# One 32-token expert item moved from the second expert group into the first, two blocks behind its 96-token item

## The chip, the cores and the metric

The kernel runs on one core of a Trainium2 chip. The metric is the device time of one execution in microseconds (us), lower is better. Before the change it took 2199.92 us (median of 3 runs, 2199.86 to 2200.71).

## The reference

The program is a chain of two transformer blocks over 256 tokens of width 1024. The change touches one step of it, the mixture of experts at the end of the first block:

```
def _moe(h, router, w1, w3, w2):
    hf = h.reshape(b * t, d)
    logits = (hf @ router).astype(jnp.float32)
    top_v, top_i = lax.top_k(logits, TOP_K)            # TOP_K = 2
    top_w = jax.nn.softmax(top_v, axis=-1)
    gates = jnp.sum(jax.nn.one_hot(top_i, N_EXPERTS) * top_w[..., None], axis=-2)
    y = jnp.zeros_like(hf)
    for e in range(N_EXPERTS):                         # 8 experts, D_EXPERT = 3584
        y = y + gates[:, e:e + 1] * _swiglu(hf, w1[e], w3[e], w2[e])
    return y.reshape(b, t, d)
```

`_swiglu` is (silu(h w1) * (h w3)) w2. Everything is in f32. Each token goes to two of the eight experts, so the kernel gathers for each expert the tokens that chose it and computes those alone. Which expert has many tokens and which few is known only on the chip.

## The kernel before

**Items and halves.** An item is one expert with room for a number of tokens. The eight experts are ranked by load, and item number i takes the expert whose rank is `SLOT_PLACE[i]`, with room `PLACE_CAPS`. In the code a room of 96 is `MIDDLE`, 160 is `LARGE`, 64 is `LOW`, 32 is `SMALL`. An expert's weights are 42 MiB, and they are streamed from HBM in 42 pieces of 1 MiB that the code calls halves. Halves 0 to 23 of an item belong to blocks 0 to 2 of w1 and w3 (8 halves a block: 4 of w1, 4 of w3), halves 24 to 27 to the short block 3, and halves 28 to 41 to w2 (the downs). The tokens are the stationary operand, 32 columns at a time, and the weights are the moving one. So PE's time for a half grows with the room of the item, and the time of its transfer doesn't.

**Places.** SyncE (SP) issues the halves in the order in which they are used, into 14 places of 1 MiB (`half`, L898). The transfer of half n waits until half n-14 has been used (`s_half_used`). In this document the halves of the whole stage are numbered through from 0: 336 of them, 42 for each of eight items.

**Groups.** Four groups and a last item are worked off in turn:

| group | items before | halves |
|---|---|---|
| first | 96 | 0 to 41 |
| second | 96 and 32 | 42 to 125 |
| third | 160 and 32 | 126 to 209 |
| fourth | 96 and 64 | 210 to 293 |
| last | 96 (a loop, here one pass) | 294 to 335 |

A group of two items takes block 0 of its first item, block 0 of its second, block 1 of the first and so on, and the downs by fives in turn (`order`). Within it PE does other work at fixed halves: the turning of the `put` table (L1371, after half 4 of a group), the turning of the inner values of each block, needed for w2 (`turn`, L1386 to L1390, two or three halves after a block), the gather of the next group's tokens into PSUM (`gather`, L979, after the 6th down half) and the scatter of the previous group's output (`scatter`, L1362, after half 1 of a group). ACT copies gathered tokens to SBUF (`tokens`, L1998), DVE makes the tables for the next group (`select`), and both do silu and the products between up and down.

Up products are at L1435 (rooms or parts of 64) and L1439 (parts of 32), the down products at L1460 and L1464.

Of the kernel before, what the change touches and what calls it, by code (L numbers as in the profile page):

```python
# [11 lines left out]
ALU = mybir.AluOpType  # L12
# [27 lines left out]
SLOT_PLACE = (0, 2, 6, 1, 7, 3, 5, 4)  # L40
# [46 lines left out]
def block_halves(block):  # L87
    return 8 if block < UP_BLOCKS - 1 else 4
# [16 lines left out]
class Group:  # L105
# [10 lines left out]
    put_parts: int  # L116

# [19 lines left out]

    def order(self):

        out = []  # L140
        for block in range(UP_BLOCKS):
            for j in range(len(self.members)):
                out += [(j, 8 * block + m) for m in range(block_halves(block))]
# [12 lines left out]

    def event(self, block, p):

        return block * len(self.parts()) + p

    def cross(self, block, p):

        small = self.small_parts()
        return block * len(small) + small.index(p)
# [4 lines left out]
    def turn_before(self, block, p):  # L169

        own = self.event(block, p)
        users = [self.event(b, q) for b in range(block + 1) for q in range(len(self.parts())) if self.turn[q] == self.turn[p]]
        return max((u for u in users if u < own), default=None)
# [5 lines left out]
def one(first, widths, up1, up3, turn, down, gathered=(0, 1), put_parts=None):  # L179
# [4 lines left out]
GROUPS = (one(0, MIDDLE, (0, 1), (2, 3), (4, 5), (6, 7), (6, 7)),  # L184
          Group(1, (MIDDLE, SMALL), (0, 1, 1), (2, 3, 3), (4, 5, 4), (7, 2, 3), (2, 3, 4, 5), (0, 1), (2, 3, 2), 3),
# [4 lines left out]
FLUSH_AT, ADD_AT, PUT_AT, PUT_SB_AT, SELECT_AT, GATHER_AFTER = 1, 3, 4, 5, 12, 5  # L190

# [189 lines left out]
def build(nc, A, out):  # L381

    with ExitStack() as ctx:
# [17 lines left out]
        s_silu_zero = sem("silu_zero")  # L401
# [29 lines left out]
        s_pad_zero = sem("pad_zero")  # L431
# [67 lines left out]
        s_gather_ready = sem("gather_ready")  # L499
        s_xg_ready = sem("xg_ready")  # L500
# [9 lines left out]
        s_y_zero = sem("y_zero")  # L510
# [295 lines left out]
        def _(sp):  # L806
# [94 lines left out]
            for g, grp in enumerate(GROUPS):  # L901
                n0 = before(halves_of, g)
                if g == 1:
                    sp.wait_ge(s_items_ready, 2)
                ids = [0 if grp.first + j == 0 else
                       sp.value_load(item_list[0:1, grp.first + j:grp.first + j + 1], min_val=0, max_val=N_EXPERTS - 1)
                       for j in range(len(grp.members))]
# [64 lines left out]
        def _(pe):  # L972
# [42 lines left out]
            pe.wait_ge(s_ones_ready, 1)  # L1015
# [328 lines left out]
            def gather(g, grp):  # L1344

                pe.wait_ge(s_select_ready, g + 1)
                cap = grp.cap()
                per = grp.per_bank()
                for k in range(KT):
                    b, at = grp.gathered[k // per], cap * (k % per)  # L1350
                    mm = group(psum[:, b, at:at + cap], [(h_tok[:, t, k * P:(k + 1) * P], pick[:, t, 0:cap]) for t in range(2)])
                mm.then_inc(s_gather_ready, 1)

# [39 lines left out]
            def experts(g, grp, ev, cr, hv, arrived, previous, following):  # L1393
# [93 lines left out]
            gather(0, GROUPS[0])  # L1487
# [251 lines left out]
        def _(act):  # L1739
# [39 lines left out]
            act.wait_ge(s_silu_zero, 1)  # L1779
# [9 lines left out]
            act.wait_ge(s_ones_ready, 1)  # L1789
# [26 lines left out]
            act.wait_ge(s_pad_zero, 1)  # L1816
# [175 lines left out]
            def tokens(g, grp):  # L1992

                act.wait_ge(s_gather_ready, g + 1)
                cap, per = grp.cap(), grp.per_bank()
                for k in range(KT):
                    b, at = grp.gathered[k // per], cap * (k % per)
                    a = act.activation(x_full[:, k, 0:cap], psum[:, b, at:at + cap], ACT.Identity, bias=mod[:, 1, 24 + k, 0:1])  # L1998
                    if k % 2:
                        a.then_inc(s_xg_ready, 1)  # L2000

# [18 lines left out]
            def experts(g, grp, ev, cr, hv, previous, following):  # L2020

                parts = grp.parts()
                for at, (j, m) in enumerate(grp.order()):
# [24 lines left out]
                    for block in range(UP_BLOCKS):  # L2048
                        for q in range(len(parts)):
                            if at == grp.turn_at(block, q):  # L2050
                                inner_turned(grp, block, q, ev)
                    if at == grp.downs() + GATHER_AFTER and following:
                        tokens(g + 1, following)

            act.wait_ge(s_items_ready, 1)
            tokens(0, GROUPS[0])
# [169 lines left out]
        def _(dve):  # L2226
# [58 lines left out]
            dve.memset(silu_c[:, :, :], 0.0).then_inc(s_silu_zero, 1)  # L2285
# [89 lines left out]
            dve.wait_ge(s_pad_zero, 1)  # L2375
# [254 lines left out]
            for t in range(2):  # L2630
                for part, width in enumerate(MIDDLE):
                    x = select_put(t, part, width, 64 * part, rank8[:, t, 0:1], gate8[:, t, 0:1])
            x.then_inc(s_put_first, 1)
# [77 lines left out]
            dve.tensor_scalar(item_rank2, item_rank, float(P), None, ALU.subtract)  # L2711
            dve.tensor_scalar(sink8, pr("sinks"), 1.0 / SCALE2, None, ALU.mult)
# [26 lines left out]
            def experts(g, grp, ev, cr, hv, previous, following, following_first):  # L2739

                parts = grp.parts()
                for at, (j, m) in enumerate(grp.order()):
# [4 lines left out]
                    for block in range(UP_BLOCKS):  # L2747
                        width = sub_block(block)
                        for q in range(len(parts)):
                            done = grp.up_done(parts[q][0], block, 0)  # L2750
                            if at == done + 1 and parts[q][1] == 32:
                                dve.wait_ge(s_half_used, hv + done + 1)
                                s = grp.cross(block, q)
                                if s:
                                    last = (block, grp.small_parts()[-2]) if q == grp.small_parts()[-1] and len(grp.small_parts()) > 1 else (
                                        block - 1, grp.small_parts()[-1])
                                    dve.wait_ge(s_up_silu, ev + grp.event(*last) + 1)
# [19 lines left out]
            dve.wait_ge(s_y_zero, 1)  # L2777
# [255 lines left out]
        def _(pool):  # L3033
            pool.memset(apad, 0.0).then_inc(s_pad_zero, 1)
# [3 lines left out]
            pool.memset(y_T, 0.0).then_inc(s_y_zero, 1)  # L3038
# [148 lines left out]
```

## Time and profile before

| what | value |
|---|---|
| median of three runs | 2199.92 us |
| span of the profiled execution | 2198.8 us |
| PE busy over the span | 2113.4 us (96%) |
| the expert stage, first to last half on PE | 811.46 to 1688.60 us of the span |
| PE busy in the second group | 175.56 of 194.96 us |

Times in rows are microseconds from the span's start. Each matmul in f32 stands in the profile as two records, so a count of x16 in a profile row is eight matmuls of the program. Nearly 4 matmuls run beside each other, in different columns of the array, so the difference between the starts of two rows is the pace, and the busy time of a row is somewhat longer than that.

### The profile page before, as it was taken

How to read it: one execution, taken by the hardware profiler on the slowest of the kernel's cores; microseconds unless marked ns; L12 is line 12 of the kernel's file. 1: busy time of each engine (PE TensorE's matmuls, PEld its weight loads, DVE VectorE, ACT ScalarE, POOL GpSimd, SP SyncE). 2: the span in 40 equal slices, each digit the busy share in tenths (PEclk: the TensorE clock that was granted, in tenths of full speed). 3: DMA queues.
4: the chain of work that ended last, by engine and by line, in shares of the span. 5: the costliest groups of instructions: out<-in, count | busy, mean ns of one | idle time of the engine just before them, and what ended most of it. 6: DMA issues, size and time to landing. Idle time of an engine off the chain costs nothing.

```text
span 2198.8 us, 35772 instructions
## 1 busy us (share of the span) xinstructions
PE 2113.4 (96%) x15146; PEld 1315.2 (60%) x15146; DVE 859.6 (39%) x1582; ACT 548.2 (25%) x1019; POOL 89.9 (4%) x109
## 2 busy tenths in 40 slices
PE   5999999999999999999889999999999999999998
PEld 2655688888866673433333343333433877889998
DVE  4698632224543432032001210110022467666755
ACT  3214432224442420010000100000011134434443
POOL 0000000000000000000000000000501200001300
PEclk9999999999999999999999999999999999999999
DMA  9895232323111559999999999999995332344451
GB/s 370 324 360 214 77 99 93 106 85 105 57 63 51 203 195 373 358 383 402 418 413 409 385 401 382 404 402 418 412 407 210 128 116 77 115 154 174 174 188 58
DMA packets 160740, 536.71 MB, mean 244 GB/s; under 512 B 7120, under 2 KB 31824, under 8 KB 139728
## 3 DMA queue, kind: packets, MB, share of 16 engines
q1 hardware_dynamic: 160448, 534.08, 63.6%
q8 instruction: 109, 1.79, 0.3%
q0 software_dynamic: 144, 0.52, 0.1%
q14 instruction: 39, 0.32, 0.0%
HBM read 533.53 MB, written 1.05 MB: 243 GB/s over the span
## 4 chain that ended last, share of the span: by engine, by line
PE 84%; DVE 6%; DMA 5%; DVEq 3%; issue 1%; ACT 1%; SPq 0%; ACTq 0%
PE psum L1435 15%; PE psum L986 11%; PE psum L987 10%; PE psum L988 10%; PE psum L979 10%; PE psum L1439 7%; PE psum L1460 7%; PE psum L1464 3%; DMA X<-in_o_exp_w 2%; DVE region L2369 2%; DVEq L2372 1%; PE psum L1003 1%; DMA region<-in_o_exp_w 1%; PE psum L1362 1%; DMA ring<-in_o_exp_w 1%
## 5 line engine op out<-in xcount | busy, mean ns | idle before, releaser
L986 PE MATMUL psum<-region_r 128*128 128x512 f32 (+1 forms) x1392 | 480.5, 345 | 14.5 <-DVE H_lo L2356 3.5
L987 PE MATMUL psum<-region_r 128*128 128x512 f32 (+1 forms) x1280 | 431.2, 337 | 0.0
L988 PE MATMUL psum<-region_r 128*128 128x512 f32 (+1 forms) x1152 | 394.4, 342 | 0.0
L986 PEld LDWEIGHTS psum<-region_r 128*128 128x128 f32 x1392 | 264.1, 190 | 62.6 <-issue 22.1
L987 PEld LDWEIGHTS psum<-region_r 128*128 128x128 f32 x1280 | 243.0, 190 | 25.3
L988 PEld LDWEIGHTS psum<-region_r 128*128 128x128 f32 x1152 | 218.5, 190 | 25.5
L1435 PE MATMUL psum<-ring,region 128*32 128x512 f32 (+1 forms) x2064 | 203.5, 527 | 1.6 <-DMA ring<-in_o_exp_w 1.6
L1435 PEld LDWEIGHTS psum<-ring,region 128*32 128x32 f32 x2064 | 65.9, 111 | 118.5 <-issue 102.7
L979 PE MATMUL psum<-H,ring 128*128 128x256 f32 x576 | 128.7, 380 | 0.0
L2008 ACT ACTIVATE region<-psum 128x256 f32<-128x256 f32 (+2 forms) x56 | 24.8, 450 | 374.8 <-PE psum L1386 277.9
L979 PEld LDWEIGHTS psum<-H,ring 128*128 128x128 f32 x576 | 108.3, 190 | 16.5 <-ACT region L2084 1.3
L1435 PE MATMUL psum<-region 128*32 128x512 f32 (+1 forms) x1072 | 115.8, 562 | 0.0
L2722 DVE COPY rstd<-psum 128x512 f32<-128x512 f32 x5 | 3.5, 692 | 277.7 <-PE psum L1464 216.5
L2735 DVE COPY region<-psum 64x512 f32<-64x512 f32 (+1 forms) x56 | 35.1, 627 | 187.6 <-PE psum L1439 186.9
L2772 DVE TENSOR_TENSOR region<-region,psum 128x512 f32<-128x512 f32 (+1 forms) x28 | 17.0, 620 | 226.3 <-PE psum L1439 184.3
L1439 PE MATMUL psum<-ring,region 128*32 128x512 f32 (+1 forms) x912 | 98.4, 525 | 0.8 <-DMA ring<-in_o_exp_w 0.8
L2369 DVE SCALAR_TENSOR_TENSOR region<-region,param 128x512 f32<-128x512 f32 x120 | 84.8, 748 | 4.1 <-issue 0.4
L2453 DVE TENSOR_TENSOR region_r<-ring,region_r 128x512 fp32r<-128x512 f32 x88 | 58.7, 689 | 57.3 <-ACT region_r L1869 57.3
L1460 PE MATMUL psum<-ring,region 128*32 128x512 f32 x640 | 77.8, 618 | 2.8 <-DMA ring<-in_o_exp_w 2.8
L1439 PE MATMUL psum<-region 128*32 128x512 f32 (+1 forms) x584 | 70.0, 571 | 4.5 <-DMA region<-in_o_exp_w 3.9
L1435 PEld LDWEIGHTS psum<-region 128*32 128x32 f32 x1072 | 33.4, 110 | 66.3 <-issue 62.4
L1869 ACT ACTIVATE region_r<-ring 128x512 fp32r<-128x512 f32 x88 | 52.8, 627 | 63.6 <-PE psum L988 63.4
(403 smaller groups left out, 2719.0 us busy)
## 6 DMA issues: line engine op xcount, KB each, us to landing
ring<-in_o_exp_w SPq DMA_DIRECT2D x151, 1024.0 KB, 12.7
region<-in_o_exp_w SPq DMA_DIRECT2D x118, 1024.0 KB, 14.3
ring<-in_w_ada SPq DMA_DIRECT2D x24, 2048.0 KB, 10.6
H<-in_o_exp_w SPq DMA_DIRECT2D x46, 1024.0 KB, 14.9
ring<-in_w_ff SPq DMA_DIRECT2D x16, 2048.0 KB, 8.0
ring<-in_e_ffn_w SPq DMA_DIRECT2D x22, 1024.0 KB, 7.8
X<-in_o_exp_w SPq DMA_DIRECT2D x21, 1024.0 KB, 14.4
ring<-in_w_in SPq DMA_DIRECT2D x10, 2048.0 KB, 8.2
```

What stands on the lines that cost most here:

```text
L979: mm = pe.matmul(dst, lhsT, rhs, start=(i == 0), stop=(i == len(pairs) - 1))
L986: pe.matmul(out, a_hi, b_hi, start=first, stop=False)
L987: pe.matmul(out, a_hi, b_lo, start=False, stop=False)
L988: mm = pe.matmul(out, a_lo, b_hi, start=False, stop=last)
L1435: mm = pe.matmul(psum[r:r + 32, to, 0:width], x_full[:, k, slot0 + 32 * tg:slot0 + 32 * tg + 32], moving, start=(k == 0), stop=(k == KT - 1))
L1439: mm = pe.matmul(psum[r:r + 32, to, 0:width], x_full[:, k, slot0:slot0 + 32], moving, start=(k < 2), stop=(k >= KT - 2))
L1460: mm = pe.matmul(psum[r:r + 32, grp.down[q], :], he[:, i, slot0 + 32 * tg:slot0 + 32 * tg + 32], moving, start=(i == 0), stop=(i == ET - 1))
L1464: mm = pe.matmul(psum[r:r + 32, grp.down[q], :], he[:, i, slot0:slot0 + 32], moving, start=(i < 2), stop=(i >= ET - 2))
L1869: act.activation(fw_hi[:, u % SPLIT, :].rearrange("p (k w n) -> p k w n", k=2, w=2), up_unit(cs, u), ACT.Copy).then_inc(s_ffn_hi, 1)
L2369: x = dve.scalar_tensor_tensor(conv[i], apad[:, i, :, k:k + T], taps[:, i, k:k + 1], conv[i], ALU.mult, ALU.add)
L2453: dve.tensor_tensor(lo, up_unit(cs, u), hi.bitcast(F32), ALU.subtract).then_inc(s_ffn_lo, 1)
L2735: dve.tensor_copy(cross_sum[0:64, to, 0:width], psum[64:128, b, 0:width])
```

## The change

The second group's 32-token item goes into the first group, and the second group is left with its 96-token item alone. The ranks of items 1 and 2 are swapped in `SLOT_PLACE`, so that the same experts keep the same rooms. The first group is now 96 and 32, with halves 0 to 83, the second 96, with halves 84 to 125. From half 126 on nothing is moved.

In the first group the second item is two blocks behind (`lag` 2): blocks A0, A1, A2, then B0, A3, B1, B2, B3 (A the 96-token item, B the 32-token one), then the downs by fives as before. B's tokens get a gather of their own after half 12, into PSUM bank 6 (`gather_second`), with a copy by ACT (`tokens_second`) and tables made by DVE behind the planning of the items, after which DVE now reports `s_put_first`. DVE's `select` for the next group waits for that gather too. SP reads B's expert number when it comes to half 24. Some semaphores are merged to make room for two new ones.

```diff
-SLOT_PLACE = (0, 2, 6, 1, 7, 3, 5, 4)
+SLOT_PLACE = (0, 6, 2, 1, 7, 3, 5, 4)
+    def up_order(self):
+        steps = [(j, step - self.lag * j) for step in range(UP_BLOCKS + self.lag) for j in range(len(self.members))]
+        return [(j, block) for j, block in steps if 0 <= block < UP_BLOCKS]
-GROUPS = (one(0, MIDDLE, (0, 1), (2, 3), (4, 5), (6, 7), (6, 7)),
-          Group(1, (MIDDLE, SMALL), (0, 1, 1), (2, 3, 3), (4, 5, 4), (7, 2, 3), (2, 3, 4, 5), (0, 1), (2, 3, 2), 3),
+GROUPS = (Group(0, (MIDDLE, SMALL), (0, 1, 1), (2, 3, 3), (4, 5, 4), (7, 2, 3), (2, 3, 4, 5), (6, 7), (2, 3, 2), 3, 2),
+          one(2, MIDDLE, (0, 1), (2, 3), (4, 5), (7, 2)),
+SECOND_AT, SECOND_BANK = 12, 6
...
+                    if g == 0 and (j, m) == (1, 0):
+                        sp.wait_ge(s_items_ready, 2)
+                        ids[1] = sp.value_load(item_list[0:1, 1:2], min_val=0, max_val=N_EXPERTS - 1)
...
+            def gather_second(grp):
+                slot0, cap = sum(grp.members[0]), grp.cap()
+                width = cap - slot0
+                pe.wait_ge(s_put_first, 1)
+                for k in range(KT):
+                    mm = group(psum[:, SECOND_BANK, width * k:width * k + width],
+                               [(h_tok[:, t, k * P:(k + 1) * P], pick[:, t, slot0:cap]) for t in range(2)])
+                mm.then_inc(s_second_gather, 1)
...
+                    if grp.lag and (j, m) == (1, 0):
+                        pe.wait_ge(s_second_xg, 1)
...
+                    if at == SECOND_AT and grp.lag:
+                        gather_second(grp)
...
+            def tokens_second(grp):
+                act.wait_ge(s_second_gather, 1)
+                for k in range(KT):
+                    a = act.activation(x_full[:, k, slot0:cap], psum[:, SECOND_BANK, width * k:width * k + width], ACT.Identity,
+                                       bias=mod[:, 1, 24 + k, 0:1])
+                a.then_inc(s_second_xg, 1)
...
-            x.then_inc(s_put_first, 1)
...
+            for t in range(2):
+                x = dve.tensor_scalar(pick[:, t, slot0:cap], cn("iota")[:, 0:cap - slot0], item_rank[:, t, 1:2], item_mask[:, t, 1:2],
+                                      ALU.is_equal, ALU.mult)
+            for t in range(2):
+                x = select_put(t, len(MIDDLE), cap - slot0, 0, item_rank[:, t, 1:2], item_gate[:, t, 1:2])
+            x.then_inc(s_put_first, 1)
...
+                        if grp.lag:
+                            dve.wait_ge(s_second_gather, 1)
```

The first place is PE's stream around half 12 (`region`, `H` and `X` are places for weights; half 13 is in `H`). Before (L1435 and L1439 are the up products of one half):

```order
L1435 MATMUL psum<-region 32x512 x8
L1439 MATMUL psum<-region 32x512 x4
L1435 MATMUL psum<-region 32x512 x8
L1439 MATMUL psum<-region 32x512 x4
L1435 MATMUL psum<-H,region 32x512 x8
L1439 MATMUL psum<-H,region 32x512 x4
```

Now (the up products are L1462 and L1466, the gather's helper L993):

```order
L1462 MATMUL psum<-region 32x512 x8
L1466 MATMUL psum<-region 32x512 x4
L1462 MATMUL psum<-region 32x512 x8
L1466 MATMUL psum<-region 32x512 x4
L993 MATMUL psum<-region 128x32 x16
L1462 MATMUL psum<-H,region 32x512 x8
L1466 MATMUL psum<-H,region 32x512 x4
```

Sixteen matmuls with 32 moving columns have come in between halves 12 and 13 of the first group.

The second place is PE's stream from half 22 of the first group on, `ring` and `region` being places for the weights. Before, block 3 of the 96-token item (256 columns) follows its block 2:

```order
L1435 MATMUL psum<-ring,region 32x512 x8
L1439 MATMUL psum<-ring,region 32x512 x4
L1435 MATMUL psum<-ring,region 32x512 x8
L1439 MATMUL psum<-ring,region 32x512 x4
L1435 MATMUL psum<-ring,region 32x256 x16
L1439 MATMUL psum<-ring,region 32x256 x8
L1435 MATMUL psum<-region 32x256 x16
L1439 MATMUL psum<-region 32x256 x8
```

Now the eight halves of B0 stand between them, four matmuls each, with the turning of A2 (L1411 to L1415) after the second:

```order
L1462 MATMUL psum<-ring,region 32x512 x8
L1466 MATMUL psum<-ring,region 32x512 x8
L1466 MATMUL psum<-region 32x512 x4
L1411 MATMUL psum<-const,region 128x128 x4
L1466 MATMUL psum<-region 32x512 x4
L1413 MATMUL psum<-const,region 128x64
L1415 MATMUL psum<-const,region 128x64 x3
L1466 MATMUL psum<-H,region 32x512 x4
L1466 MATMUL psum<-X,region 32x512 x4
L1466 MATMUL psum<-H,region 32x512 x4
L1466 MATMUL psum<-region 32x512 x8
L1462 MATMUL psum<-region 32x256 x16
```

The first block of short halves, which followed half 49, now follows half 23.

## Rows read from the trace of the kernel before

**Rows 1.** Busy time by group (stretch, length, engines, granted clock, DMA share, GB/s).
```profile
811.46:929.96 118.50, 118.50 (x1172) 43.69 (x1176) 23.21 (x65) 13.23 (x32) 0.00 (x0) 1.00 0.95 353
929.96:1124.92 194.96, 175.56 (x1596) 61.59 (x1589) 34.65 (x64) 16.73 (x37) 0.00 (x0) 0.95 1.01 403
1124.92:1365.82 240.90, 240.22 (x2361) 88.84 (x2365) 34.47 (x62) 18.53 (x42) 0.00 (x0) 0.99 1.00 395
1365.82:1573.76 207.94, 207.19 (x2040) 79.72 (x2032) 24.87 (x45) 17.09 (x38) 25.62 (x42) 1.00 1.02 409
```
**Rows 2.** What PE waited for from 1126 to 1689 us (total, times, longest).
```profile
PE psum L1460 <- DVE region L2772: 0.7, 1, 0.7
```
**Rows 3.** PE timeline of the first group (start, length, line, shapes, count).
```profile
806.95 3.78 PE L979 MATMUL psum<-region 128*128 128x96 f32 x32
...
814.06 1.90 PE L1435 MATMUL psum<-H,region 128*32 128x512 f32 x16
...
816.63 1.90 PE L1435 MATMUL psum<-region 128*32 128x512 f32 x16
...
824.47 0.66 PE L1371 MATMUL psum<-const,region 128*128 128x128 f32 x4
...
877.06 1.91 PE L1435 MATMUL psum<-ring,region 128*32 128x256 f32 x32
...
905.57 3.84 PE L979 MATMUL psum<-region 128*128 128x128 f32 x32
```
**Rows 4.** SP timeline: issue of the transfer into the first freed place.
```profile
814.30 0.37 SPq L898 DMA_DIRECT2D X<-in_o_exp_w  x1
```
**Rows 5.** DMA issues from 857 to 877 us (KB, us from issue to landing).
```profile
ring<-in_o_exp_w SPq DMA_DIRECT2D x4, 1024.0 KB, 6.8
```
**Rows 6.** PE timeline of the second group, with idle time before a row and its releaser.
```profile
935.23 3.72 PE L1362 MATMUL psum<-region,rstd 64*128 64x256 f32 x32
...
946.74 0.87 PE L1371 MATMUL psum<-const,region 128*128 128x128 f32 x6
...
962.11 1.04 PE L1439 MATMUL psum<-X,region 128*32 128x512 f32 x8
962.97 1.04 PE L1439 MATMUL psum<-H,region 128*32 128x512 f32 x8
...
1022.26 1.94 PE L1439 MATMUL psum<-region 128*32 128x512 f32 x8 [1.48 <-DMA region<-in_o_exp_w]
1024.83 1.94 PE L1439 MATMUL psum<-region 128*32 128x512 f32 x8 [0.62 <-DMA region<-in_o_exp_w]
...
1029.95 1.07 PE L1439 MATMUL psum<-ring,region 128*32 128x512 f32 x8 [0.78 <-DMA ring<-in_o_exp_w]
1032.66 3.42 PE L1435 MATMUL psum<-ring,region 128*32 128x256 f32 x32 [1.64 <-DMA ring<-in_o_exp_w]
...
1054.15 1.92 PE L1460 MATMUL psum<-X,region 128*32 128x512 f32 x16 [1.58 <-DMA X<-in_o_exp_w]
...
1068.63 5.47 PE L979 MATMUL psum<-region 128*128 128x192 f32 x32
...
1104.88 3.64 PE L1460 MATMUL psum<-ring,region 128*32 128x512 f32 x16 [1.42 <-DMA ring<-in_o_exp_w]
```
**Rows 7.** PE timeline where the third group begins.
```profile
1124.92 5.08 PE L1435 MATMUL psum<-X,region 128*32 128x512 f32 x32 [1.58 <-DMA X<-in_o_exp_w]
...
1130.68 3.62 PE L1435 MATMUL psum<-H,region 128*32 128x512 f32 x32
...
1140.47 3.64 PE L1435 MATMUL psum<-region 128*32 128x512 f32 x32
1144.78 3.62 PE L1435 MATMUL psum<-region 128*32 128x512 f32 x32
```
**Rows 8.** DVE timeline: `put` tables of the first item, and the end of the planning.
```profile
808.02 1.12 DVE L2627 TENSOR_SCALAR region<-const,small 128x128 f32<-128x128 f32 x4
...
818.85 0.16 DVE L2713 TENSOR_TENSOR gain<-param 128x8 f32<-128x8 f32 x1
```

More of the change, by code:

```diff
@@ L116 @@
     put_parts: int
+    lag: int = 0
     def parts(self):
@@ L136, in per_bank @@
         return next(n for n in (8, 4, 3, 2) if n <= fit)
+    def up_order(self):
+        steps = [(j, step - self.lag * j) for step in range(UP_BLOCKS + self.lag) for j in range(len(self.members))]
+        return [(j, block) for j, block in steps if 0 <= block < UP_BLOCKS]
     def order(self):
         out = []
-        for block in range(UP_BLOCKS):
-            for j in range(len(self.members)):
-                out += [(j, 8 * block + m) for m in range(block_halves(block))]
+        for j, block in self.up_order():
+            out += [(j, 8 * block + m) for m in range(block_halves(block))]
         for m0 in range(UP_HALVES, HALVES, DOWN_RUN):
@@ L155, in up_done, with events, crosses @@
         return self.at(j, 8 * block + block_halves(block) // 2 * (mat + 1) - 1)
+    def events(self):
+        return [(block, p) for j, block in self.up_order() for p in self.of_member(j)]
+    def crosses(self):
+        return [(block, p) for block, p in self.events() if p in self.small_parts()]
     def event(self, block, p):
-        return block * len(self.parts()) + p
+        return self.events().index((block, p))
     def cross(self, block, p):
-        small = self.small_parts()
-        return block * len(small) + small.index(p)
+        return self.crosses().index((block, p))
     def turn_at(self, block, p):
@@ L171, in turn_before @@
         own = self.event(block, p)
-        users = [self.event(b, q) for b in range(block + 1) for q in range(len(self.parts())) if self.turn[q] == self.turn[p]]
+        users = [self.event(b, q) for b, q in self.events() if self.turn[q] == self.turn[p]]
         return max((u for u in users if u < own), default=None)
@@ L902, in _ @@
                 n0 = before(halves_of, g)
-                if g == 1:
-                    sp.wait_ge(s_items_ready, 2)
-                ids = [0 if grp.first + j == 0 else
+                ids = [0 if g == 0 else
                        sp.value_load(item_list[0:1, grp.first + j:grp.first + j + 1], min_val=0, max_val=N_EXPERTS - 1)
@@ L1343, in _, with gather @@
             stay_busy(1, SHIFT_BANK)
-            def gather(g, grp):
+            def gather(g, grp, width=None):
                 pe.wait_ge(s_select_ready, g + 1)
                 cap = grp.cap()
+                width = width or cap
                 per = grp.per_bank()
@@ L1350, in gather @@
                     b, at = grp.gathered[k // per], cap * (k % per)
-                    mm = group(psum[:, b, at:at + cap], [(h_tok[:, t, k * P:(k + 1) * P], pick[:, t, 0:cap]) for t in range(2)])
+                    mm = group(psum[:, b, at:at + width], [(h_tok[:, t, k * P:(k + 1) * P], pick[:, t, 0:width]) for t in range(2)])
                 mm.then_inc(s_gather_ready, 1)
+            def gather_second(grp):
[6 more added lines that the diff above has]
+                mm.then_inc(s_second_gather, 1)
             def scatter(flushed, n_parts, banks):
@@ L1486, in _ @@
             pe.wait_ge(s_htok_sb, 4)
-            gather(0, GROUPS[0])
+            gather(0, GROUPS[0], sum(GROUPS[0].members[0]))
             for g, grp in enumerate(GROUPS):
@@ L1815, in _ @@
             weights_hi(1)
-            act.wait_ge(s_pad_zero, 1)
+            act.wait_ge(s_zeroed, 1)
             for m in range(Z_GROUPS):
@@ L2051, in experts @@
                                 inner_turned(grp, block, q, ev)
+                    if at == SECOND_AT and grp.lag:
+                        tokens_second(grp)
                     if at == grp.downs() + GATHER_AFTER and following:
@@ L2631, in _ @@
                 for part, width in enumerate(MIDDLE):
-                    x = select_put(t, part, width, 64 * part, rank8[:, t, 0:1], gate8[:, t, 0:1])
-            x.then_inc(s_put_first, 1)
+                    select_put(t, part, width, 64 * part, rank8[:, t, 0:1], gate8[:, t, 0:1])
             def select(grp, first):
@@ L2754, in experts @@
                                 if s:
-                                    last = (block, grp.small_parts()[-2]) if q == grp.small_parts()[-1] and len(grp.small_parts()) > 1 else (
-                                        block - 1, grp.small_parts()[-1])
-                                    dve.wait_ge(s_up_silu, ev + grp.event(*last) + 1)
+                                    dve.wait_ge(s_up_silu, ev + grp.event(*grp.crosses()[s - 1]) + 1)
                                 both_rows(0, grp.up1[q], width).then_inc(s_up_cross, 1)
```

32 lines of the change are left out of this document (18 added, 14 removed).

## The prediction

> **What bounds the kernel now.** I read the stage in four views, in this order.
>
> First the busy times by group [rows 1]. In the first group PE is busy all of its 118.50 us while the DMA queues move 353 GB/s. In the second PE is busy 175.56 of 194.96 us, and the queues move 403 GB/s at a share of 1.01. In the third and fourth PE is busy but for 0.7 us each. So the transfers bound the second group and PE all others.
>
> Then the waits. From half 126 on PE waits for nothing but two products of DVE, 0.7 us each (one row stands for both) [rows 2]. Whatever moves the start of half 126 therefore moves the end of the program by as much, and nothing else in this change can, since the work behind it is the same.
>
> Then PE's timeline. A half of the 96-token item takes 816.63 - 814.06 = 2.57 us [rows 3], one of a 32-token item 0.86 us, and a transfer 2.57 us too (the distance of two halves that PE waited for) [rows 6]. Full places are a reserve that the short halves eat at 1.7 us each, until PE waits. In the second group this ends in the waiting rows, the last at half 126, at 1124.92 [rows 7]: that start is a landing.
>
> Last SP's issues. In the first group a place is refilled when PE frees it: half 0 is done at 814.06 and half 14 issued at 814.30 [rows 3, 4]. PE's extra work there (turning, gather) is lost to the queues. That is the 353 against 403 GB/s: 118.5 x (1 - 353/403) = 14.7 us of transfer time, which is what one would hope to win.
>
> **The change part by part.** The last wait moves from half 126 to half 84, the end of the new first group. I work out when half 84 lands, and then what PE has to do from there to half 128, where the work is as before (its start was 1140.47 [rows 7]).
>
> *The start.* Nothing ahead of half 0 changes on PE. DVE's report for the `put` table now waits for the planning, which ended at 818.85 + 0.16 = 819.0. Behind it stand four more instructions; four `put` tables took 1.12 us [rows 8], so it comes at about 820.1. PE asks for it after half 4, at 824.47 [rows 3]. Cost nothing; if the planning took 4 us more, each further microsecond would be one of PE.
>
> *Three parts instead of two in the first `put` turning.* 0.87 against 0.66 us [rows 6, 3]: +0.2 us.
>
> *The second gather.* 16 matmuls with 32 moving columns. No row shows that shape. The gather of 96 columns took 3.78 us, of 128 3.84 us, of 192 5.47 us [rows 3, 6]. Below 128 columns the width hardly counts. Bounds: by width alone 3.78/3 = 1.3 us, and as much as 128 columns, 3.8 us. I take 3.7, on the line of the two nearest rows. It stands between halves 12 and 13 with nothing beside it on PE. ACT's eight copies have eleven halves until B0 needs them, and DVE's `select`, now behind that gather, serves a gather 50 halves later: nothing. ACT's and DVE's later work is queued behind both, but the first turned values are needed two blocks later.
>
> *SP.* The read of B's expert number comes with the transfer of half 24, which waits for half 10, eleven halves of 2.57 us into the group and so beyond 839. The list is ready before 819: nothing.
>
> *The landing of half 84.* Half 24 began at 877.06 [rows 3], now at 877.06 + 0.2 + 3.7 = 881.0. At that moment the place for half 37 is free: issued 0.25 later, landed 6.8 after that [rows 4, 5], at 888.0. From there short halves free places faster than the queues fill them, and transfers follow each other without a gap. Halves 38 to 51 are 14 at 2.57 = 36.0 [rows 6]. Halves 52 to 55, the short block, are 4 at 1032.66 - 1029.95 = 2.71, 10.8 [rows 6]. Half 56, the first down, takes 70.8/28 = 2.5. From 56 to 84 it is the same mix as from 98 to 126 before, 1124.92 - 1054.15 = 70.8 [rows 6, 7]. Sum 888.0 + 36.0 + 10.8 + 2.5 + 70.8 = 1008.1.
>
> Does PE wait there? From half 24 on it has 18 halves at 2.57 and 42 at 0.86, and its turning and gather (in the old first group these were 118.5 - 42 x 2.57 = 10.6 us, taken as an estimate here), 93 us in all. Half 84 lands 127 us after that: yes, also if its waits on DVE grow between B1, B2 and B3, which now follow each other directly. Those hide behind the same transfers.
>
> Bounds of the landing: 1.3 us less if half of the 2.57 us that a transfer may stand behind its neighbour drops out of the 6.8. 2.2 us more if the 47 halves from 38 to 84 go at the old second group's mean, 1.0486 MB at 403 GB/s or 2.60 us each [rows 1], 122.3 instead of 120.1.
>
> *The second group, now PE's.* It has the halves of the old first group, 118.5 us [rows 1]. Added are the scatter of three parts and the wider gather. The scatter is 1140.47 - 1130.68 less a half of 4.31, 5.5 us [rows 7]. The gather is 192 instead of 128 columns, 5.47 - 3.84 = 1.6 us [rows 6, 3].
>
> *The clock behind the wait.* After short waits in the second group the first eight matmuls of a half took 3.64 instead of 1.90 us [rows 6, 3], and half 126 took 5.76 instead of 4.31 [rows 7]; the group's granted clock is 0.95 [rows 1]. That is the lower of the two levels, 1.2 GHz. The same would meet half 84: +1.7 us, bounds 0 and 2.6 (a whole half at 1.2 GHz). The cost of 1.5 us that stood at half 126 goes.
>
> [...]
>
> So half 126 begins at 1008.1 + 1.7 + 118.5 + 5.5 + 1.6 = 1135.4 instead of 1124.92. Two halves of 4.31 [rows 7] and a scatter of now two parts, 3.7 [rows 6], bring half 128 to 1147.7, against 1140.47: **+7.2 us**.
>
> Behind it the places fill sooner in the third group (PE is 20 us behind the landings at its start instead of 0), SP waits more, and that costs nothing: in the old third group, too, PE came to hold the queues back (395 against 403 GB/s [rows 1]).
>
> Why does the saved transfer time not come out? The group that follows needs 127 us of PE for 106 us of transfers. Before, that PE time lay in the first group, where it also had nothing beside it. The change moves the wait and doesn't remove it. It removes cover: the turning of A0 and A1 and the wide gather lay inside the stretch that waits for transfers, and now lie outside. To this comes a gather of 3.7 us.
>
> The profiled execution spans 2198.8 us, 1.1 below the median of 2199.9. I add 7.2 to the median: **2207.1 us**.
>
> **The rivals.**
>
> *A, faster: the transfers bound both groups.* If the second group followed the landings as it does now, half 126 would land at 1008.1 + 24 x 2.57 + 4 x 2.71 + 14 x 2.53 = 1116, 9 us before 1124.92, and the time would be 2191. For it speaks the DMA share of 1.01 in the old second group. Against it: the same 42 halves took PE 118.5 us without any wait [rows 1], and would have to take 108. It decides from there: each microsecond of PE over 108 behind half 84 is lost, and at 118 the gain is gone. Chance 0.07.
>
> *B, no change: the terms come low together.* The gather costs 1.3 (-2.4), half 84 lands 1.3 earlier because the queues catch up a part of the gather's delay, and the clock costs nothing (-1.7): +1.8, 2201.7. Half of this gives 2204.4. For it speaks that the queues ran at 353 of 403 GB/s where the gather stands [rows 1], against it that all three must go one way. Chance 0.18.
>
> *C, slower still: the clock stays low.* The first group now waits through 20 short halves in a row and then in each round of downs. If the last round, four A and four B halves, ran at 1.2 GHz throughout, it would take 4 x 5.1 + 4 x 1.7 = 27 us against 20 of transfers, and PE would reach half 84 7 us late: 2214. Against it: the old second group had the same rounds, and PE still waited at the end of each. Chance 0.07.
>
> My forecast has the remaining 0.68, with a range of its own from 2203.5 to 2210.5 (the bounds: -1.3 and +2.2 of the landing, -1.7 and +0.9 of the clock, -2.4 and +0.1 of the gather, taken about three quarters).
>
> **How the numbers follow.** What this kernel's measurement can tell from no change is 0.2%, 4.4 us: above 2204.3 is slower, below 2195.5 faster. Slower: C, 0.9 of the forecast's 0.68 and a fifth of B's 0.18, together 0.72. Faster: A, 0.07. The rest, 0.21, is the same. The range goes from 2200 to 2211.5. It leaves out A, most of C and the ends of the others.
>
> **What would show it.** In the changed profile:
> - 16 matmuls of 128x32 after half 12, 3.7 us.
> - The first group, halves 0 to 83, ends at about 1008, with PE idle in it some 20 us or more, all before DMA landings, the first of them around half 45.
> - The second group's 42 halves are without a wait for a DMA, and take 127 us. Half 126 begins near 1135, 10 us later than before, half 128 near 1148.
> - From there to the end the distance stays.
>
> The forecast is wrong if PE waits for DMA in the new second group (then A), if half 84 begins before 1004 or if the second gather is near 1 us (B), or if half 84 lands several us before PE takes it (C).

## The result, and the profile after

The changed kernel takes 2211.77 us (median of 4, 2209.36 to 2214.48) against 2199.89 us of the kernel before in the same comparison (4 runs, 2196.91 to 2200.71). The ratio is 1.0057, with an interval from 1.0045 to 1.0069: slower, by 11.9 us. The forecast was +7.2 us and 2207.1 us, in a range up to 2211.5. The sign and the mechanism are as forecast, the size is not, and the time lies just above the range.

The profiled execution after spans 2208.6 us, 9.8 more than before: the stage is 11.9 longer, what stands ahead of it 3.6 shorter and what stands behind it 1.5 longer. Outside the stage PE's work is the same in both kernels: half 0 begins at 807.86 here and between 807.7 and 809.6 in the seven profiles below, whatever the kernel, and only in the profile of before at 811.46 [rows 1]. So from here on I count time from the start of half 0, and write it with a plus sign (+197.8 is 197.8 us after half 0). Each such number is the start of a half in PE's timeline less the start of half 0. That the stage and the medians differ by the same 11.9 is partly chance, since each profile is one execution.

The busy times by group after (stretch, length, PE, PEld, DVE, ACT, POOL, granted clock, DMA share, GB/s) answer to [rows 1]:

```profile
807.86:1005.63 197.77, 178.56 (x1593) 60.51 (x1594) 36.40 (x86) 19.52 (x51) 0.00 (x0) 0.91 0.97 381
1005.63:1136.39 130.76, 128.73 (x1221) 50.49 (x1224) 20.84 (x42) 11.05 (x25) 0.00 (x0) 0.98 1.02 410
1136.39:1374.09 237.70, 237.02 (x2349) 86.83 (x2345) 35.14 (x63) 19.13 (x43) 0.00 (x0) 1.00 0.94 364
```

The first group is now the one bound by transfers (PE idle for 19.2 us), and the second is PE's. Its queues move 410 GB/s while PE works: the transfers of the third group run ahead. In the third group they then drop to 364, since the places are full. As forecast, the idle time has changed groups and not gone.

PE's timeline where the second group begins (start, length, line, shapes, count, idle time and its releaser), answering to [rows 7]:

```profile
1000.44 1.06 PE L1491 MATMUL psum<-region 128*32 128x512 f32 x8 [1.43 <-DMA region<-in_o_exp_w]
1002.96 1.06 PE L1491 MATMUL psum<-H,region 128*32 128x512 f32 x8 [1.45 <-DMA H<-in_o_exp_w]
1005.63 3.64 PE L1462 MATMUL psum<-X,region 128*32 128x512 f32 x16 [1.60 <-DMA X<-in_o_exp_w]
1009.01 1.96 PE L1466 MATMUL psum<-X,region 128*32 128x512 f32 x8
1010.72 2.29 PE L1462 MATMUL psum<-H,region 128*32 128x512 f32 x16
1012.82 1.04 PE L1466 MATMUL psum<-H,region 128*32 128x512 f32 x8
```

Half 84 is the first of these rows at L1462, and nothing behind it waits for a DMA. It lands at +197.8 (forecast +196.6) and takes 1010.72 - 1005.63 = 5.09 us instead of 2.57, twice as long: the granted clock was 0.50 in every microsecond from 1005 to 1011, the lower of the two levels. Half 85 begins slowly, too.

PE's timeline where the third group begins:

```profile
1136.39 3.62 PE L1462 MATMUL psum<-X,region 128*32 128x512 f32 x32
...
1145.09 3.72 PE L1387 MATMUL psum<-region,rstd 64*128 64x256 f32 x32
1148.74 1.49 PE L1462 MATMUL psum<-region 128*32 128x512 f32 x12
```

Half 126 (1136.39, no wait ahead of it) is at +328.5, half 128 (1148.74) at +340.9 against 1140.47 - 811.46 = +329.0 before: 11.9 us later. At the stage's last half, 335, the distance is still 11.9 (+886.4 against +874.5). The whole loss arises ahead of half 128, as forecast; behind it nothing is lost and nothing is won back. From half 128 to half 335 it takes 545.5 us in both kernels, and in all seven profiles below but the last (546.0).

What PE waited for from 1137 to 1697 us (total, times, longest), answering to [rows 2]:

```profile
PE psum L1487 <- DVE region L2818: 0.7, 1, 0.7
PE psum L1466 <- DVE region L2818: 0.7, 1, 0.7
```

Two places hold time that the forecast didn't have. The first is behind the second gather (PE's timeline):

```profile
844.09 3.82 PE L993 MATMUL psum<-region 128*128 128x32 f32 x32
847.84 3.50 PE L1462 MATMUL psum<-H,region 128*32 128x512 f32 x16
851.16 1.03 PE L1466 MATMUL psum<-H,region 128*32 128x512 f32 x8
```

The same in the busy times of two stretches of 4 us (columns as above):

```profile
844.00:848.00 4.00, 4.00 (x40) 3.85 (x40) 0.00 (x0) 0.06 (x1) 0.00 (x0) 0.96 1.01 403
848.00:852.00 4.00, 4.00 (x24) 0.87 (x24) 1.60 (x6) 1.48 (x8) 0.00 (x0) 0.62 0.23 88
```

Half 13, right behind the gather, takes 852.02 - 847.84 = 4.18 us instead of 2.57, at a granted clock of 0.62, though PE had not been idle (in every microsecond from 848 to 851 it was 0.50, the lower level). (852.02 is the start of the next row.) The second place is the start of w2 in the second group:

```profile
1088.93 1.91 PE L1462 MATMUL psum<-H,region 128*32 128x256 f32 x32
1090.66 1.05 PE L1466 MATMUL psum<-H,region 128*32 128x256 f32 x16
1093.73 1.93 PE L1487 MATMUL psum<-X,region 128*32 128x512 f32 x16 [2.03 <-issue]
```

PE stands still for 2 us ahead of half 112, for which the profile names no releaser ("issue"). DVE's timeline over the same stretch names it:

```profile
1091.77 0.42 DVE L2818 TENSOR_TENSOR region<-region,psum 128x256 f32<-128x256 f32 x1 [5.79 <-PE psum L1466]
...
1093.22 0.42 DVE L2818 TENSOR_TENSOR region<-region 64x256 f32<-64x256 f32 x1
```

DVE's last product of block 3 ends at 1093.64, and PE's matmul starts 0.09 us later. The group's tuple tells why: in `one(2, MIDDLE, (0, 1), (2, 3), (4, 5), (7, 2))` the second pair of banks is w3's products, the last pair the downs, and bank 2 is in both. DVE reads it for the part of 64 (1091.77) and then has three more instructions for the part of 32. PE's one wait ahead of w2 (on `s_eh_ready`) stands on the last of them.

### The profile page after: what moved, and what is told of

Read it like the earlier page. It is cut to its first block, busy times and chain, and to the rows that moved or that the text cites. A ratio compares the mean times of both kernels' runs of the same rounds, so it can differ in the third digit from the quotient of the medians.

```text
span 2208.6 us, 35845 instructions
## 1 busy us (share of the span) xinstructions
PE 2125.5 (96%) x15178; PEld 1321.6 (60%) x15178; DVE 859.9 (39%) x1582; ACT 549.9 (25%) x1027; POOL 89.9 (4%) x109
## 4 chain that ended last, share of the span: by engine, by line
PE 84%; DVE 6%; DMA 5%; DVEq 3%; issue 1%; ACT 1%; SPq 0%; ACTq 0%
PE psum L1462 16%; PE psum L1000 10%; PE psum L1001 10%; PE psum L1002 10%; PE psum L993 10%; PE psum L1466 7%; PE psum L1487 7%; PE psum L1491 3%; DMA X<-in_o_exp_w 2%; DVE region L2411 2%; DVEq L2414 1%; PE psum L1017 1%; DMA region<-in_o_exp_w 1%; PE psum L1387 1%; DMA ring<-in_o_exp_w 1%
## 5 line engine op out<-in xcount | busy, mean ns | idle before, releaser
L1462 PE MATMUL psum<-ring,region 128*32 128x512 f32 (+1 forms) x1984 | 194.5, 524 | 0.0
L1462 PEld LDWEIGHTS psum<-ring,region 128*32 128x32 f32 x1984 | 62.9, 110 | 110.4 <-issue 97.2
L993 PE MATMUL psum<-H,ring 128*128 128x256 f32 x576 | 128.7, 380 | 0.0
L993 PEld LDWEIGHTS psum<-H,ring 128*128 128x128 f32 x576 | 108.3, 190 | 16.5 <-ACT region L2126 1.3
L1462 PE MATMUL psum<-region 128*32 128x512 f32 (+1 forms) x1104 | 117.7, 556 | 0.0
L1466 PE MATMUL psum<-ring,region 128*32 128x512 f32 (+1 forms) x904 | 103.9, 553 | 4.2 <-DMA ring<-in_o_exp_w 4.2
L1462 PEld LDWEIGHTS psum<-region 128*32 128x32 f32 x1104 | 34.3, 110 | 67.0 <-issue 62.4
L993 PE MATMUL psum<-region 128*128 128x128 f32 (+6 forms) x488 | 71.3, 299 | 0.7 <-ACT region L2197 0.6
L1466 PE MATMUL psum<-region 128*32 128x512 f32 (+1 forms) x592 | 69.2, 561 | 1.4 <-DMA region<-in_o_exp_w 0.8
## 6 DMA issues: line engine op xcount, KB each, us to landing
ring<-in_o_exp_w SPq DMA_DIRECT2D x151, 1024.0 KB, 12.3
```

The source lines that it names most:

```text
L993: mm = pe.matmul(dst, lhsT, rhs, start=(i == 0), stop=(i == len(pairs) - 1))
L1462: mm = pe.matmul(psum[r:r + 32, to, 0:width], x_full[:, k, slot0 + 32 * tg:slot0 + 32 * tg + 32], moving, start=(k == 0), stop=(k == KT - 1))
L1466: mm = pe.matmul(psum[r:r + 32, to, 0:width], x_full[:, k, slot0:slot0 + 32], moving, start=(k < 2), stop=(k >= KT - 2))
```

## The experiments

There are two theories. The first is the forecast's: what PE does behind the last wait for a DMA counts in full, what it does within the waiting stretch (the halves over which PE waits for transfers again and again) is covered, and what it does ahead of it, with the places full, delays the landings one for one. The rival: the 11.9 us are local stalls (bank 2, the clock behind the gather, the turning two blocks late), without which the new order would be as good as the old.

### Other banks in the second group

```
-          one(2, MIDDLE, (0, 1), (2, 3), (4, 5), (7, 2)),
+          one(2, MIDDLE, (0, 1), (3, 6), (4, 5), (7, 2)),
```

> Base: the changed kernel. In the new second group one half takes 4.80 instead of 2.60 us, the last before w2, since its down products go to bank 2, which its up products also use, and so PE waits for DVE's product. Here the up products of w3 go to banks 3 and 6, and the down products stay in 7 and 2. Theory (the wait stands on a path bounded by PE): that half takes 2.6 us, half 126 begins 2.2 us earlier after half 84, the whole 2.2 us less than the changed kernel. Rival (DVE is late anyway and PE meets it at the next half or turning): the 2.2 us stay.

Measured: 2207.72 us (2206.24 to 2210.82), 1.0037 of before [1.0023, 1.0051]. PE's timeline at the start of w2:

```profile
1091.67 1.05 PE L1466 MATMUL psum<-H,region 128*32 128x256 f32 x16
1092.53 1.90 PE L1487 MATMUL psum<-X,region 128*32 128x512 f32 x16
```

The wait is gone; from half 111 to half 112 it takes 2.59 us instead of 4.80. That is -2.2 us at this place, shown, and nothing takes it back: from half 86 to half 126 it is 115.0 us here and in the run with all three repairs, and 117.2 in the four profiles of this order with the old banks. The whole stage is only 1.4 us shorter (+885.0), since half 84 began at +199.6 here; the median says -4. Both lie within what separates single executions from each other (the changed kernel's own four times differ by 5 us).

### The second gather in four pieces

The 16 matmuls stand in fours behind halves 9 to 12 instead of all behind half 12.

```
+                for k in (2 * part, 2 * part + 1):
...
-                    if at == SECOND_AT and grp.lag:
-                        gather_second(grp)
+                    if SECOND_AT - 3 <= at <= SECOND_AT and grp.lag:
+                        gather_second(grp, at - SECOND_AT + 3)
```

> Base: the changed kernel. The second gather (16 matmuls of 32 columns) is split into four pieces of four matmuls, behind halves 9, 10, 11 and 12. Theory (the run of narrow matmuls lets PE's clock fall, granted 0.62 behind it, half 13 at 4.18 instead of 2.58 us, and whatever PE loses there reaches half 84): the pieces together take 3.8 to 4.2 us, no half behind them is slow, half 84 begins 1.6 us earlier counted from half 0, the whole -1.3 to -1.6 us. Rival (the slow half has another cause, such as the restart of the weight stream): four restarts instead of one, the same or up to 1 us slower.

Measured: 2208.53 us (2206.97 to 2212.39), 1.0041 [1.0027, 1.0056]. PE's timeline there:

```profile
847.34 1.08 PE L993 MATMUL psum<-region 128*128 128x32 f32 x8
848.35 1.92 PE L1463 MATMUL psum<-H,region 128*32 128x512 f32 x16
850.09 1.04 PE L1467 MATMUL psum<-H,region 128*32 128x512 f32 x8
```

Four matmuls take 1.0 us in this row. The four pieces together delay half 13 by 4.1 us, the whole gather did it by 3.9, so the pieces save nothing of the gather itself, but no half is slow any more, and half 24 begins at +70.2 instead of +71.6. Half 84 began at +198.3 all the same, not 1.6 us earlier as expected. What moved the end of this profile was half 84 itself, which took 2.57 us: no fall of the clock behind the last wait. The median is 3.2 us below the changed kernel's, but this profile doesn't show that the 1.6 us behind the gather reach the end.

### One block of lag instead of two

```
-GROUPS = (Group(0, (MIDDLE, SMALL), ..., (6, 7), (2, 3, 2), 3, 2),
+GROUPS = (Group(0, (MIDDLE, SMALL), ..., (6, 7), (2, 3, 2), 3, 1),
```

> Base: the changed kernel. The 32-token item follows one block behind instead of two: A0, A1, B0, A2, B1, A3, B2, B3. Theory (half 84 lands when PE's start of the first short half, plus the lag of a transfer, plus an unbroken row of transfers says): short halves begin at half 16 instead of 24, the turning of A1 falls into the stretch that waits for transfers, half 84 begins 195.9 us after half 0 instead of 197.8, the whole -1.5 to -2 us. Rival (the later the short halves begin, the more 96-token work is left to cover transfers): slower by about 1 us.

Measured: 2210.79 us (2206.8 to 2211.49), 1.0049 [1.0033, 1.0066]. Half 84 lands at +197.2 (after: +197.8; expected +195.9) and half 126 at +326.4. PE's timeline at half 84:

```profile
1005.07 1.93 PE L1462 MATMUL psum<-X,region 128*32 128x512 f32 x8 [1.59 <-DMA X<-in_o_exp_w]
```

The median is only 1.0 us below the changed kernel's, and the profiled execution was the fastest of the four (2206.8, the others 2210.6 to 2211.5). So one profile cannot settle 1.9 us here. Over all six profiles of this order half 84 begins at +197.8, +199.6, +198.3 and +198.4 with two blocks of lag (mean 198.5), and at +197.2 and +196.1 with one (mean 196.65). The difference of 1.9 agrees with the theory, with only two profiles on one side. The spread of about 1 us around each mean is the noise of one profile.

### The gather alone, in the kernel before

16 matmuls of the second gather's shape are added to the kernel before, behind half 10 of its first group; their output is not used.

```
+                    if at == 10 and not previous:
+                        for k in range(KT):
+                            group(psum[:, 6, 32 * k:32 * k + 32], [(h_tok[:, t, k * P:(k + 1) * P], pick[:, t, 0:32]) for t in range(2)])
```

> Base: the kernel before. Sixteen matmuls of 32 moving columns, as in the second gather, are added behind half 10 of the first group, into a free bank; nobody reads them. PE waits 19 us for transfers later in this kernel, in the second group. Theory (work on PE while all places are full delays the transfers by as much, and the later wait gives nothing back): 3.8 us for the matmuls and about 1.6 us of low clock behind them, half 126 begins 5 to 5.5 us later counted from half 0, the whole +5 us. Rival (the later wait absorbs it): half 126 begins at the same time, +0 us.

Measured: 2202.01 us (median of 10), 1.0015 [1.0004, 1.0026]. PE's timeline behind half 10 and at half 126:

```profile
838.77 3.76 PE L979 MATMUL psum<-region 128*128 128x32 f32 x32
842.46 1.92 PE L1435 MATMUL psum<-region 128*32 128x512 f32 x16
...
1124.39 1.94 PE L1435 MATMUL psum<-X,region 128*32 128x512 f32 x8 [0.82 <-DMA X<-in_o_exp_w]
```

Busy times of this kernel's second group:

```profile
930.38:1124.39 194.01, 175.72 (x1597) 61.45 (x1590) 34.65 (x64) 16.41 (x37) 0.00 (x0) 0.94 1.01 401
```

Half 24 begins 3.8 us later than before (+69.4 against +65.6), half 126, 102 halves on and behind 194.01 - 175.72 = 18.3 us of waits, 2.9 later (+316.3 against +313.5), the last half 3.0 later. By the ratio the whole is 3.3 us longer, with an interval from 0.9 to 5.7. Expected were 5 us, 1.6 of them from a low clock behind the gather; here the clock didn't fall, and of the gather's own 3.8 us 2.9 came through. The waits of the second group do not absorb the work that stands ahead of them, or a small part of it. That contradicts the reading "PE has idle time later, so this is free" and speaks for the first theory; that the delay is one for one it doesn't show, with about 1 us of noise in each landing.

### Short halves first in the second group, in the kernel before

If what counts is PE's work up to the first short halves, they should come sooner. In the kernel before, the second group takes block 0 of the 32-token item ahead of block 0 of the 96-token item (B0 A0 B1 A1 ...). PE's work is the same.

```
+    def up_order(self):
+        return [(j, b) for b in range(UP_BLOCKS) for j in sorted(range(len(self.members)), reverse=bool(self.lead))]
...
-        for block in range(UP_BLOCKS):
-            for j in range(len(self.members)):
-                out += [(j, 8 * block + m) for m in range(block_halves(block))]
+        for j, block in self.up_order():
+            out += [(j, 8 * block + m) for m in range(block_halves(block))]
...
-          Group(1, (MIDDLE, SMALL), ..., (0, 1), (2, 3, 2), 3),
+          Group(1, (MIDDLE, SMALL), ..., (0, 1), (2, 3, 2), 3, 1),
```

The numbering of the events and the waits on them follow this order.

> Base: the kernel before, items and groups as there. In the second group the 32-token item goes first in each pair of blocks: B0, A0, B1, A1, B2, A2, B3, A3; downs as before. Theory (half 126 lands at PE's start of the first short half, plus about 8 us, plus an unbroken row of transfers): the first short half is half 42 instead of 50, the scatter and the first turning of the group fall into the stretch that waits for transfers, and half 126 begins 5 us earlier counted from half 0 (308 instead of 313.5 us), the whole 2195 us, faster than before by 0.2%. PE waits as long or longer in the group. Rival (the reserve is eaten in any case and only the amount of 96-token work in the group counts): half 126 within 1 us of before.

Measured: **2196.03 us** (median of 11, 2194.39 to 2197.18) against 2199.06 of the kernel before (16 runs), 0.9985 [0.9976, 0.9994]: faster than both kernels. The busy times of the first two groups answer to [rows 1]:

```profile
808.70:927.23 118.53, 118.53 (x1176) 43.72 (x1180) 23.19 (x65) 13.23 (x32) 0.00 (x0) 1.00 0.95 355
927.23:1118.20 190.97, 174.71 (x1598) 61.90 (x1591) 34.62 (x64) 16.32 (x37) 0.00 (x0) 0.95 1.02 409
```

PE's timeline at half 42 and at half 126:

```profile
927.20 1.04 PE L1450 MATMUL psum<-X,region 128*32 128x512 f32 x8
928.06 1.04 PE L1450 MATMUL psum<-H,region 128*32 128x512 f32 x8
...
1118.19 1.08 PE L1446 MATMUL psum<-X,region 128*32 128x512 f32 x4 [0.73 <-DMA X<-in_o_exp_w]
```

The first group is as long as before (118.53 against 118.50), the second 4.0 us shorter: half 126 is at +309.5 instead of +313.5 (expected +308), the stage's last half 3.7 earlier. The queues moved 409 instead of 403 GB/s in the second group; that places come free sooner is the likely reason, and not measured. One expectation failed: PE waits less in the group, not as long or longer (190.97 - 174.71 = 16.3 us against 19.4), so most of what the group gained was waiting.

### The three repairs together

The banks, the gather in pieces and one block of lag, all in the changed kernel (its diff is the sum of the first three).

> Base: the changed kernel with three edits together: up products of the second group in banks 3 and 6, the second gather in four pieces behind halves 9 to 12, one block behind instead of two. Theory (three separate costs on one path): -2.2, -1.4 and -1.7 us, half 126 begins about 323.5 us after half 0 (328.5 in the changed kernel, 313.5 before), the whole 2206 us, so still 5 us or more slower than the kernel before, because the group behind the last wait has 127 us of PE work instead of none. Rival (the small costs were the loss): 2200 to 2202 us.

Measured: 2205.96 us (2204.64 to 2209.0), 1.0031 [1.0018, 1.0043]. Half 84 is at +196.1 and half 126 at +323.8: 4.7 us before the changed kernel's +328.5, as expected, and still 10.4 us behind the +313.5 of before. Of the 4.7 us 2.2 are the banks, 1.7 the landing of half 84, and 0.8 lie between halves 84 and 86, where the clock differs from one execution to the next. PE's timeline at half 84:

```profile
1005.64 2.79 PE L1463 MATMUL psum<-X,region 128*32 128x512 f32 x12 [0.72 <-DMA X<-in_o_exp_w]
```

At half 128 the distance to the kernel before is 7.2 us (+336.2 against +329.0), since that kernel has its low clock and its scatter of three parts between halves 126 and 128 (15.5 us against 12.3). By the medians it is 7 us. So with bank 2 and the gather's stall mended the order still loses. The rival theory accounts for a part of the difference between forecast and result (the 2.2 us of the banks for certain), but not for the loss itself.

### The second gather with 128 columns

The changed kernel, with 128 instead of 32 moving columns in the second gather, into banks 6 and 7; of the output the same 32 are used.

```
-                               [(h_tok[:, t, k * P:(k + 1) * P], pick[:, t, slot0:cap]) for t in range(2)])
+                               [(h_tok[:, t, k * P:(k + 1) * P], pick[:, t, 0:128]) for t in range(2)])
```

> Base: the changed kernel. The second gather is made with 128 moving columns instead of 32 (all four slots of 32, of which the last is used), in one piece, into two banks: same number of matmuls and weight loads, four times the columns. Theory (it was the small share of streaming in that run that let the clock fall): the gather takes 3.9 us, half 13 behind it 2.6 instead of 4.18 us, the granted clock stays 1.00. Rival (the clock falls behind any such run at that place, or by chance): half 13 stays at 3.9 to 4.2 us.

Measured: 2210.28 us (2 runs, 2209.49 and 2211.06), 1.005 [1.0031, 1.0068]. PE's timeline there:

```profile
843.94 3.84 PE L993 MATMUL psum<-region 128*128 128x128 f32 x32
847.71 1.92 PE L1463 MATMUL psum<-H,region 128*32 128x512 f32 x16
849.45 1.04 PE L1467 MATMUL psum<-H,region 128*32 128x512 f32 x8
```

Four times the columns cost nothing (3.84 against 3.82 us), and half 13 is back at 2.6 us. But half 84 began at +198.4 and half 126 at +328.9, no earlier than in the changed kernel (+197.8, +328.5). The 1.6 us are gained at half 13 and not found at half 84. Either the queues had made them up by then, or the noise of 1 us around half 84 hides them; which of the two stays open.

## Why the prediction failed in size and held in kind

Four steps held.

*The second gather* was priced at 3.7 us from the gathers of 96 and 128 columns, against a bound of 1.3 by width. It took 3.8 (844.09 to 847.84). The weight loads take the time: PEld is busy 3.85 of the 4 us from 844 to 848. 32 records in 3.82 us are 119 ns each, at 32 columns as at 128 (3.84 us). The Trainium skill, "TensorE: Matmul & The Clock Gate", section "LDWEIGHTS (loading the stationary operand)", says that a load takes about P / 1.2 ns, P being the columns of the stationary operand. For the 128 columns here that is an estimate of 107 ns, and the spacing of 119 ns agrees within 12%; the load records themselves overlap and last 193 ns in the mean.

*The landing of half 84*, forecast at +196.6, came at +197.8, and at +198.5 in the mean of four profiles. Both are later than forecast and within the stated bound of 2.2 us.

*PE's idle time* in the first group was 19.2 us ("some 20", said to be all for DMA landings; about 2 of them are not: 1.6 stand ahead of w2, as in the second group, and 0.6 behind a product of DVE), the second group had no wait for a DMA, and *from half 128 to the end* the distance stayed. So rival A, in which the transfers bound both groups, is out: the second group took PE 130.8 us. Rival B needed a cheap gather and an early half 84, and had neither. Rival C, the clock low through the last round before half 84, is out too. The four 96-token downs of that round (halves 76 to 79) took 2.57 us each, and PE still waited 1.60 us for half 84. Their first and last row:

```profile
985.55 1.92 PE L1487 MATMUL psum<-ring,region 128*32 128x512 f32 x16 [0.90 <-DMA ring<-in_o_exp_w]
...
993.30 1.90 PE L1487 MATMUL psum<-ring,region 128*32 128x512 f32 x16
```

*Only what PE does ahead of the waiting stretch or behind it counts* is borne out from both sides: by work added ahead of it (+3.8 us there, +2.9 at half 126) and by the short halves put first (-4.0).

The terms that were mis-sized add up to 4.6 of the 4.7 us between +7.2 and +11.9. The last column has the mean over profiles of the new order: those with two blocks of lag for the landing, those with the old banks for halves 86 to 126, and all six for the rest:

| step | forecast | measured | missing | mean of like profiles |
|---|---|---|---|---|
| landing of half 84 | +196.6 | +197.8 | 1.2 | +198.5 (4) |
| halves 84 to 86: two halves, clock, scatter | 12.3 | 13.5 | 1.2 | 12.5 (6) |
| halves 86 to 126: "it has the halves of the old first group, 118.5" | 115.0 | 117.2 | 2.2 | 117.2 (4) |
| halves 126 to 128 | 12.3 | 12.3 | 0 | 12.3 (6) |

By the means 4.3 us are missing, nearly all in the landing (1.9) and in the second group (2.2).

The step that failed most is *the second group, now PE's*. I took the old first group's 118.5 us for the same 42 halves. But that group had banks 6 and 7 for its downs, and this one has 7 and 2, with bank 2 shared with an up product. The item's matmuls are the same, its banks aren't, and DVE's product came between: a wait that the sum put at nothing. The bank experiment shows the 2.2 us: with other banks halves 86 to 126 take 115.0, the forecast's number. The number stood in the tuple that the change writes, so it could have been seen.

*The clock behind the wait*: forecast 1.7 us with a bound of 2.6. Half 84 cost 2.5 more, and half 85, which began slowly, 0.4: 1019.18 (half 86) less 1005.63 is 13.55 us, 5.4 of them the scatter at its usual pace. The bound was right in kind but too near, since I let the low clock end with the half. But from half 84 to half 86 this profile is the slowest of six: in the others of the same order half 84 took 4.54 (banks), 2.57 (gather in pieces), 3.88 (one block of lag), 4.73 (all three) and 5.09 us (128 columns). The mean is 4.3, or 1.7 above the pace, which is what was forecast. So this term varies from one execution to the next and was sized rightly; its 1.2 us in the table are chance.

*The landing of half 84*: half 24 was forecast at +69.5 and began at +71.6. Of the 2.1 us 1.6 are the slow half behind the gather; the rest is the turning, which now stands in two places for each block instead of one (0.78 + 0.85 us instead of 1.51 for block 0), and 0.2 of the gather. That the lateness of half 84 stems from this isn't shown, as the runs with the gather in pieces and with 128 columns mended half 13 and not half 84. Why half 84 lands 1.9 us late in the mean stays open.

The range was too narrow at the upper end: its bounds covered each term's known uncertainty, and none of them a wait that no row of before could show. With every bound at its upper end the sum gives 2210.3 us, still below the 2211.8 measured; and three quarters of the bounds give 2203.1 to 2209.5, not the 2203.5 to 2210.5 that the prediction writes.

## What to carry to other kernels

In a stream with a fixed number of places, find the last wait for a transfer. What PE does behind it counts in full, what it does ahead of the waiting stretch (with the places full) delays the landings almost as much (2.9 of 3.8 us here), and only what lies between the two is covered; so judge a new order by which work it moves out of that stretch, and put the short pieces early, as the fastest kernel here does with the same work. When a group's duration is carried over to a group with other buffers or banks, compare the buffers as well as the work.

## What the runs showed of the hardware that was not expected

- The granted clock fell without an idle time of PE. Behind 3.8 us of matmuls with 32 moving columns it was 0.62 (848 to 852 us), and the next half took 4.18 us; so, too, in the bank experiment (4.10) and with one block of lag (3.88). With 128 columns in the same time, and with the gather in pieces, the next half took 2.6. But the same narrow gather in the kernel before, behind half 10, was followed by a half at full pace (842.46, 1.92). So the fall came in all three profiles with the narrow gather in one piece behind half 12, and in none of the other four profiles with a second gather (in pieces, with 128 columns, in the kernel before); there is one profile of each kernel, and the cause stays open.
- A wait of 0.5 to 1.6 us for a DMA was followed by a low clock in some places and not in others. After the waits of 1.43 and 1.45 us ahead of halves 82 and 83 of the changed kernel the rows lasted 1.06 us, full pace; after 1.60 us ahead of half 84 the granted clock was 0.50, and the half took 5.09 us; and in the six profiles of this order that half took from 2.57 to 5.09.
- The start of one half behind a wait for a DMA differs by about 1 us either way between executions of like kernels (half 84 at +197.8 to +199.6), and what lies outside the stage by more: half 0 begins at 807.7 to 811.5 us, and behind the stage it takes 510.0 to 512.7. For effects below 2 us the positions in the stage, compared over several profiles, said more than one span did.
